# Routing matrix built between the expert-up tiles, and the up products parked in DRAM until the first down pass

## The reference, cut to what matters

```
qry = (hc @ w_query).reshape(-1, 8, 2, 128)
s = einsum('chpk,pnk->chpn', qry, sub_keys)
s1, i1 = top_k(s[:, :, 0], 16);  s2, i2 = top_k(s[:, :, 1], 16)
cand_s = s1[..., :, None] + s2[..., None, :]
top_s, pos = top_k(cand_s, 16)                 # 128 picks of a token
idx  = take_along_axis(i1 * 128 + i2, pos)
gate = softmax(top_s)
act  = gelu(einsum('cd,chkd->chk', hc, expert_u[idx]))
out  = einsum('chk,chkd->cd', gate * act, expert_v[idx])
```

## Time and profile before

| | us |
|---|---|
| median of 3 runs (2500.84 to 2504.45) | 2502.86 |
| the profiled execution, its own time | 2502.85 |
| its span in the profile | 2500.9 |
| PE busy, share of the span | 2391.2 (96%) |
| DVE, ACT, POOL busy | 1705.2, 1425.6, 193.2 |

### The profile page before, as it was taken

The page is one execution under the profiler, slowest core; times in us unless marked ns, Lnnn a source line. Parts: engine busy times, 40 slices in busy tenths (PEclk is TensorE's granted clock), DMA queues, the critical chain, the costliest instruction groups (busy, mean ns, idle before and its releaser), DMA issues. The chain is left out here.

```text
span 2500.9 us, 59673 instructions
## 1 busy us (share of the span) xinstructions
PE 2391.2 (96%) x19183; PEld 2338.6 (94%) x19183; DVE 1705.2 (68%) x3328; ACT 1425.6 (57%) x2560; POOL 193.2 (8%) x194
## 2 busy tenths in 40 slices
PE   8999999999999999999999999857999999999997
PEld 7999889989999999999999999756999999999997
DVE  7774688877776677777775444698666666666665
ACT  6444455556554566666666666765555555555553
POOL 0321000020110000000000000285000002000000
PEclk9999999999999999999999999899999999999999
DMA  6887444455664455555555555301666665566663
GB/s 215 288 300 240 154 150 136 135 173 173 184 209 158 153 172 179 171 177 175 175 170 182 179 183 183 111 0 58 214 181 179 182 178 169 181 179 182 179 182 119
DMA packets 121906, 431.95 MB, mean 173 GB/s; under 512 B 14568, under 2 KB 18920, under 8 KB 121584
## 3 DMA queue, kind: packets, MB, share of 16 engines
q1 hardware_dynamic: 116048, 410.08, 52.5%
q0 software_dynamic: 5792, 21.01, 2.3%
HBM read 423.28 MB, written 7.76 MB: 172 GB/s over the span
## 5 line engine op out<-in xcount | busy, mean ns | idle before, releaser
L262 DVE TENSOR_TENSOR lo<-raw,hi 128x512 fp32r<-128x512 f32 x1504 | 1034.3, 696 | 502.9 <-ACT hi L257 474.6
L257 ACT CAST hi<-raw 128x512 fp32r<-128x512 f32 x1504 | 908.9, 618 | 484.2 <-PE ps L277 359.2
L275 PE MATMUL ps<-h_hi,hi 128*128 128x264 f32 (+1 forms) x3200 | 920.4, 288 | 23.2 <-DVE lo L262 21.7
L277 PE MATMUL ps<-h_hi,lo 128*128 128x264 f32 (+1 forms) x3200 | 912.3, 285 | 0.0
L276 PE MATMUL ps<-h_lo,hi 128*128 128x264 f32 (+1 forms) x3200 | 912.1, 285 | 0.0
L275 PEld LDWEIGHTS ps<-h_hi,hi 128*128 128x128 f32 x3200 | 603.6, 189 | 38.7 <-DVE lo L262 24.1
L276 PEld LDWEIGHTS ps<-h_lo,hi 128*128 128x128 f32 x3200 | 604.0, 189 | 0.0
L277 PEld LDWEIGHTS ps<-h_hi,lo 128*128 128x128 f32 x3200 | 601.4, 188 | 0.0
L1730 PE MATMUL ps<-w_hi,hi 128*128 128x264 f32 x2048 | 584.3, 285 | 4.4 <-DVE x L1712 2.4
L1731 PE MATMUL ps<-w_lo,hi 128*128 128x264 f32 x2048 | 582.0, 284 | 0.0
L1732 PE MATMUL ps<-w_hi,lo 128*128 128x264 f32 x2048 | 581.7, 284 | 0.0
(11 more groups left out here) (264 smaller groups left out, 2317.3 us busy)
## 6 DMA issues: line engine op xcount, KB each, us to landing
raw<-u_tiles SPq DMA_DIRECT2D x256, 512.0 KB, 3.6
raw<-expert_v SPq DMA_DIRECT2D x256, 512.0 KB, 5.0
raw<-weights SPq DMA_DIRECT2D x240, 512.0 KB, 3.5
qb<-q_spill POOLq DMA_DIRECT2D x8, 512.0 KB, 7.7
x<-xT SPq DMA_DIRECT2D x4, 560.0 KB, 6.8
kvT<-qkv SPq DMA_DIRECT2D x1, 2240.0 KB, 12.6
x<-xT SPq DMA_DIRECT2D x1, 2240.0 KB, 8.7
x_spill<-x SPq DMA_DIRECT2D x1, 2112.0 KB, 8.7
```

The costliest lines, as they stand in the source:

```text
L257: nc.scalar.copy(hi[k % SPLIT][:], raw_quarter(k)).then_inc(hi_done, 1)
L262: nc.vector.tensor_tensor(lo[k % SPLIT][:], raw_quarter(k), hi[k % SPLIT][:].bitcast(F32), ALU.subtract).then_inc(lo_done, 1)
L275: pe.matmul(out, a, rh, start=start and j == 0, stop=False)
L277: m = pe.matmul(out, b, rh, start=False, stop=stop and j == QT - 1)
```

## The change: what it does

- The routing stage as a block disappears. Softmax (`soft_first`, `soft_second`), the exponential on ACT and the transposes go between the quarters of up pair `PAIR_R` (the 41st) and the one after it. The groups follow in the last 22 up pairs: 60 of them in 20 pairs, three to a pair (`G_AT`: behind quarters 0, 3 and 5), then four more in the last two pairs. Groups 64 and 65 are left for after the last tile.
- The product of a group is copied into `W` (`keep`) and not multiplied into it, since the up products are no longer there: gelu writes to one of two staging buffers `ust`, and POOL stores each tile to DRAM (`u_spill`) with a DMA of 128 x 264 numbers, 132 KB. POOL waits for each store to land before it issues the next one. The gelu of a pair waits for the store of the same buffer of the pair before (`u_free`).
- The one-hot matrices of the groups in the up pass live in the last 24 columns of `W` (`left_hot`, `right_hot`). One matrix is `W[:, :, c]`: its 128 numbers of a partition stand 264 numbers (1056 bytes) apart. Three sets of them, a ring, are in use. All right matrices are made by DVE; POOL makes none.
- In the first down pass SP loads each tile back into one of four buffers `urg`, and DVE multiplies it into `W[:, n, :]` (`times_u`) one chunk ahead of its use. In the second pass nothing is loaded.
- Some small constants change places in memory, so that the buffers fit.

```diff
-GS = 6
+GT, GR, GB = 4, 3, 6
+GP = 20
+MADE = GT * GR * GP
...
+    ust = [place(f"ust{b}", at["rows"] + 1056 * b, [P, LIVE]) for b in range(2)]
...
+    urg = place("urg", at["fin_r"], [P, 4, LIVE])
+    u_dram = nc.dram_tensor("u_spill", [NK, P, LIVE], F32, kind="Internal").ap()
...
+    PAIR_R = PAIR_QRY + PH * HEAD_PAIRS
+    PAIR_G = PAIR_R + 2
+    LEFT = (MADE + GT * 4) // GT
+    GROUPS = LIVE // GT
+    G_AT = (0, 3, 5)
+    MAKE_AT = (2, 5, 7)
...
+    def left_hot(b, t):
+        return W[:, :, MADE + 2 * GT * (GR - 1 - b) + t]
+    def right_hot(b, t):
+        return W[:, :, MADE + 2 * GT * (GR - 1 - b) + GT + t]
...
+            sp.wait_ge(mm_done, 8 * PAIR_U + SPLIT)
+            for b in range(2):
+                sp.wait_ge(u_free[b], NK // 2)
+            for s in range(4):
+                sp.dma_start(urg[:, s], u_dram[s]).then_inc(u_in[s], 16)
+        @block.gpsimd
+        def _(pool):
+            for b in range(2):
+                pool.sem_inc(u_free[b], 1)
+            with pool.Fori(0, NK // 2) as i:
+                for b in range(2):
+                    pool.wait_ge(tile_free[b], i + PAIR_QRY + 2)
+                    nc.gpsimd.dma_start(u_dram[2 * i + b], ust[b][:]).then_inc(u_out[b], 16)
+                    pool.wait_ge(u_out[b], 16 * i + 16)
+                    pool.sem_inc(u_free[b], 1)
...
+            def gelu(i, b):
+                act.wait_ge(u_free[b], i - PAIR_QRY + 1)
+                nc.scalar.activation(ust[b][:], ps[:, b, 0:LIVE], ACT.Gelu_apprx_tanh).then_inc(tile_free[b], 1)
+            def make(n, tok, out):
+                for t in range(2):
+                    nc.scalar.activation(out(t), iota[:], ACT.Square,
+                                         bias=chT[:, 3, bass.ds(tok + t, 1)]).then_inc(sq_done, 1)
+                for t in range(2):
+                    act.wait_ge(sq_done, 2 * n + t + 1)
+                    m = nc.scalar.activation(out(t), out(t), ACT.Relu, scale=-2.0,
+                                             bias=chT[:, 2, bass.ds(tok + t, 1)])
+                m.then_inc(l_act, 1)
...
+            with act.Fori(0, GP - 1) as p:
+                i = p + PAIR_G
+                for k in range(8):
+                    split_hi(act, 8 * i, AHEAD + k)
+                    if k in MAKE_AT:
+                        b = MAKE_AT.index(k)
+                        ring_make(GR * p + GR + b, b)
+                    if k % 4 == 3:
+                        tile_done(act, i, k // 4)
+                        gelu(i, k // 4)
...
+            def group(n, bank, lefts, rights):
+                pe.wait_ge(l_ready, n + 1)
+                pe.wait_ge(l_act, n + 1)
+                pe.wait_ge(g_used, n + 1)
+                for t in range(GT):
+                    m = pe.matmul(ps[:, bank, NK * t:NK * t + NK], lefts(t), rights(t), start=True, stop=True)
+                m.then_inc(g_ready, 1)
+            with pe.Fori(0, GP // 2) as p:
+                for u in range(2):
+                    i = 2 * p + u + PAIR_G
+                    for c in range(2):
+                        pe.wait_ge(tile_free[c], i + 1)
+                        for r in range(4):
+                            quarter_products(pe, 8 * i, 4 * c + r, ps[:, c, 0:LIVE], h2, QT * r, LIVE, r == 0, r == 3)
+                            if 4 * c + r in G_AT:
+                                b = G_AT.index(4 * c + r)
+                                group(2 * GR * p + GR * u + b, 2 + GR * u + b,
+                                      lambda t: left_hot(b, t), lambda t: right_hot(b, t))
...
+            def keep(n, bank):
+                dve.wait_ge(g_ready, n + GR + 1)
+                nc.vector.tensor_copy(W[:, :, bass.ds(GT * n, GT)], ps[:, bank, :].rearrange("p (t n) -> p n t", t=GT))\
+                    .then_inc(g_used, 1)
...
+                        split_lo(dve, 8 * i, AHEAD + k)
+                        if k in MAKE_AT:
...
+                            keep(n, 2 + GR * u + b)
+                            ring_make(n + GR, b)
...
                         load_half(sp, C0 + 4 * i + s, s, expert_v[0, 4 * i + s])
+                        sp.wait_ge(w_mul, 4 * i + s - 3)
+                        sp.dma_start(urg[:, s], u_dram[4 * i + s]).then_inc(u_in[s], 16)
...
+            def times_u(i, k):
+                n = 4 * i + k
+                dve.wait_ge(u_in[k % 4], 16 * (i + k // 4) + 16)
+                nc.vector.tensor_tensor(W[:, n, :], W[:, n, :], urg[:, k % 4], ALU.mult).then_inc(w_mul, 1)
```

More of the change, by code:

```diff
@@ new lines, in ring_make @@
+            def ring_make(n, b):
+                act.wait_ge(g_ready, n + 1 + late(n))
+                act.sem_inc(act_go, 1)
+                make(n, GT * n, lambda t: left_hot(b, t))
+            act_pairs(act, PAIR_QRY, PAIR_R, lambda i: gelu(i, 0), lambda i: gelu(i, 1))
+            for i in (PAIR_R, PAIR_R + 1):
+                for k in range(8):
+                    split_hi(act, 8 * i, AHEAD + k)
+                    if i == PAIR_R and k == 2:
+                        act.wait_ge(soft, 2)
+                        nc.scalar.activation(chosen[:, 2], chosen[:, 2], ACT.Exp).then_inc(soft_act, 1)
+                    if i == PAIR_R + 1 and k == 0:
+                        act.wait_ge(ch_done, 4)
+                    if i == PAIR_R + 1 and k in MAKE_AT:
+                        ring_make(MAKE_AT.index(k), MAKE_AT.index(k))
+                    if k % 4 == 3:
+                        tile_done(act, i, k // 4)
+                        gelu(i, k // 4)
@@ new lines, in _ @@
+            with act.Fori(0, GP - 1) as p:
+                i = p + PAIR_G
+                for k in range(8):
+                    split_hi(act, 8 * i, AHEAD + k)
+                    if k in MAKE_AT:
+                        b = MAKE_AT.index(k)
+                        ring_make(GR * p + GR + b, b)
+                    if k % 4 == 3:
+                        tile_done(act, i, k // 4)
+                        gelu(i, k // 4)
+            for i in range(PAIR_G + GP - 1, PAIR_U):
+                for k in range(8):
+                    split_hi(act, 8 * i, AHEAD + k)
+                    for n, b in LAST_MAKES.get((i - PAIR_G - GP, k), ()):
+                        ring_make(n, b)
+                    if k % 4 == 3:
+                        tile_done(act, i, k // 4)
+                        gelu(i, k // 4)
@@ L1417, in _ @@
+            act.wait_ge(mm_done, 8 * PAIR_U + SPLIT)
+            for n in range(LEFT, GROUPS):
+                make(n, GT * n, lambda t: lhot[:, n - LEFT, t])
         @block.tensor
         def _(pe):
-            pe_pairs(pe, PAIR_QRY, PAIR_U, h2, LIVE)
+            pe.sem_inc(g_ready, GR)
+            pe.sem_inc(g_used, GB)
+            pe_pairs(pe, PAIR_QRY, PAIR_R + 1, h2, LIVE)
+            pe.wait_ge(soft, 5)
+            for t in range(TT):
+                n = (P, P, DEC)[t]
+                for q in range(3):
+                    m = pe.transpose(ps[:, 2 + q, P * t:P * t + n],
+                                     chosen[0:n, q, t].rearrange("p h k -> p (h k)"), ident[0:n, 0:n])
@@ new lines, in _ @@
+            for i in range(PAIR_G + GP, PAIR_U):
+                for c in range(2):
+                    pe.wait_ge(tile_free[c], i + 1)
+                    for r in range(4):
+                        quarter_products(pe, 8 * i, 4 * c + r, ps[:, c, 0:LIVE], h2, QT * r, LIVE, r == 0, r == 3)
+                        for n, b in LAST_GROUPS.get((i - PAIR_G - GP, 4 * c + r), ()):
+                            group(n, 2 + n % GB, lambda t: left_hot(b, t), lambda t: right_hot(b, t))
+            for n in range(LEFT, GROUPS):
+                group(n, 2 + n % GB, lambda t: lhot[:, n - LEFT, t], lambda t: rhot[:, n - LEFT, t])
@@ L1507, in _ @@
                 assert split[0] == 8 * HEAD_PAIRS and count[0] == STEPS, (split[0], count[0], STEPS)
[L1508 to L1568, removed]
-                for q in range(3):
[L1570 to L1614, removed]
-                m.then_inc(l_ready, 1)
-            def weigh(i, b):
-                dve.wait_ge(g_ready, GS + GS * i + b + 1)
-                wv = W[:, :, bass.ds(4 * GS * i + 4 * b, 4)]
-                nc.vector.tensor_tensor(wv, wv, ps[:, 2 + b, :].rearrange("p (t n) -> p n t", t=4),
-                                        ALU.mult).then_inc(g_used, 1)
-            for b in range(GS):
-                hots(0, b)
-            with dve.Fori(0, GROUPS // GS - 1) as i:
-                for b in range(GS):
-                    weigh(i, b)
-                    hots(i + 1, b)
-            for b in range(GS):
-                weigh(GROUPS // GS - 1, b)
@@ new lines, in transposed, with make @@
+            def transposed():
+                dve.wait_ge(tr_ready, 1)
+                for q in range(3):
+                    nc.vector.tensor_copy(chT[:, q, :], ps[:, 2 + q, 0:LIVE]).then_inc(ch_done, 1)
+                dve.wait_ge(ch_done, 3)
```

(55 more changed lines are left out.)

100 lines of the change are left out of this document (70 added, 30 removed).

## The result

The changed kernel takes 2513.89 us (median of 7 runs, 2507.61 to 2515.99) against 2500.84 for the kernel before (7 runs, 2495.28 to 2504.45): a ratio of 1.0056, 95% interval 1.0045 to 1.0067. It is slower by about half a per cent, where 2462 us had been forecast.

What follows compares the result with a forecast made beforehand. PE's instructions were taken to bound both passes. From 2502.85 us, 119.6 for the gap came off; 75.5 for groups, 2.3 for transposes and 1 for joints were added: 2462.05, say 2462 us, range 2445 to 2516.

Steps and rivals of the forecast that it cites:

- part 2: 64 groups on PE's path in the up pass: 1.18 us each, 75.5 us in all (57 to 165).
- rival 1: PE pays for strided group operands, kernel slower: 2507 us at 0.087 a record, 2552 with both operands; chance 0.21.
- The DVE row: DVE reading 128 numbers: 279 ns side by side, 366 at 64 bytes' distance, 87 ns more; used for upper ends.
- The prediction's estimate from that page: If the 16-byte line rule doubled every PE group record: 512 x 0.111 = 57 us higher, 2519 us.
- the change of kind: PE going between up matmuls and float32 group matmuls: 0.29 us a group, taken from the query tiles' period.
- rival 4: Changing between matmul kinds costs nothing between long runs: 64 x 0.29 = 19 us less, 2443 us; chance 0.05.
- Part 1: Gap between up and first down pass: routing stage goes, 8.1 us of 127.7 stay, saving 119.6 us.
- the slow start: PE restarting after idling before the last two groups: 1.5 to 1.8 us a group and not 0.9.
- Part 3: DVE, ACT and POOL keep up in the up pass: DVE 10.7 us, ACT 9.0 of a 15.1 us pair; cost zero.
- rival 2: POOL's store chain sets the clock of the first 40 pairs, beyond 5.8 us a tile: 2511 us; chance 0.07.
- Part 4: Small things: nine transposes on PE's path 2.3 us, reloads in the first down pass zero, unseen joints 1 us.
- Rival 3: DVE or ACT delays splits in pairs with groups, or a late reload stalls the down pass: 2475 to 2494; chance 0.12.

Runs made afterwards that it cites:

- blocks: The changed kernel with W stored by groups of four tokens, so each one-hot matrix is 128 numbers side by side; 2443.73 us, ratio 0.9767 to the kernel before.
- both8: As blocks, but left and right matrices both interleaved, 8 bytes from number to number; 2451.37 us, a single run.
- one_product: The changed kernel with PE making only the first of a group's four products, spread over the four tokens; all matrices still made; 2419.12 us.
- blocks_x2: As blocks, but the 2.1 MB load of x2 in the first down pass cut into eight; 2440.29 us, ratio 0.9756 to the kernel before.

## Why the prediction was wrong

- **The step that failed** is the choice in part 2: "I take 75.5", a group at 1.18 us. It measured 1.99, 127.5 us in all, 52 us more. The other terms err by 1 us together (-0.3, -1.9 and +1.2), so this is nearly the whole distance between the forecast 2462.05 and the profiled execution's 2512.79. It turned a forecast gain of 41 us into a loss. The range (2445 to 2516) does hold the result, close to its upper end, since it took in the lower part of rival 1; the way the time would move was forecast wrong. The mechanism was named as rival 1, with a break-even of 0.080 us a record; the records are 0.238 apart, 0.127 above the 0.111 of the kernel before. Rival 1's own prices (2507 and 2552) hold the result between them, but it had a chance of 0.21.
- **Why the choice was wrong.** The ground for it was that a float32 record spends two cycles on a column and so leaves room for a slow read. The runs show that it leaves none: from 0.111 us side by side (blocks) the record goes to 0.227 to 0.238 with either operand at 16 bytes, or both at 16 or at 1056. The DVE row was the only strided row that the prediction had, it pointed the right way, and I set it aside because it was not PE's. It was too low as a price (0.087 a read of 128 numbers, from two lines that also write 8 sums and 16; PE's is 0.116 to 0.127), and the way it was added up was wrong too: moving and weights do not add, the slower counts.
- The Trainium skill, SBUF — State Buffer, in its note on SBUF cachelines, says that two hits to a 16-byte line give full bandwidth. By that rule both8 agrees, 0.118 us at 8 bytes against 0.236 at 16. The prediction's estimate from that page (each record doubled, 2519 us) was the nearest of all, in part by luck: it put the strides at 57 us where they cost 65 (512 x 0.127), and it kept 0.29 us a group for the change of kind, where 0.09 is left (1.99 - 8 x 0.238).
- **A second size in the same term** erred the other way. The 0.29 us for the change of kind, taken from the query tiles, is nothing between up matmuls (blocks: 0.898 us for eight records). That was rival 4, and without the strides the time would have been below the forecast: 2444. The trace of the kernel before says where the 0.29 stands. Behind the six records that start at 747.65 come

```profile
748.50 0.39 PE L275 MATMUL ps<-raw_hi,hi 128*128 128x264 f32 x1
748.72 0.29 PE L276 MATMUL ps<-raw_lo,hi 128*128 128x264 f32 x1
```

  so the six take 0.85 us to the next up matmul, and the eight of blocks 0.81. The four records of full width follow one another at 0.107 to 0.112 us, the first of them 0.120 behind the tile's matmul: going over to them costs nothing. The last two records have eight weight columns (the third matmul of L1270). 0.09 us stand ahead of them (0.205 from the fourth record to the fifth) and 0.19 behind (0.43 from the last record to the tile's second matmul, 0.24 in blocks). So the 0.29 belongs to the narrow matmul, which a group doesn't have; why a narrow one costs this was not tested.
- **Part 1 was right** in its sum: 7.78 us stay against 8.1. Inside it two errors offset each other. The two groups ran 2.74 us for 16 records, faster than the slow start I had put. That start was the clock: in the kernel before PE stood still for 4.7 us at a granted clock of 0.50 (the lower level, 1.2 GHz) and had 0.61 in the 6.1 us of the 32 records; here it stood for 1.8 us and had 0.81 in the 2.8 us of the two groups. The turn of the blocks, from the end of the last copy to the first down matmul, took 2.24 us against 1.68.
- **Part 3 was right.** In a pair with groups DVE waits 1.6 to 2.4 us for `hi` before three of its eight splits, PE waits for no `lo`, and one_product shows room down to 13.3 us. DVE is busy for 11.1 us of a pair (10.7 forecast) and ACT for 9.6 (9.0). POOL's chain is far from its bound: the stores land in 2.0 us at the median (4.3 at most) where 4.5 had been estimated from a 32 KB store's 4.1; rival 2 never came near.
- **Part 4**: transposes and joints took 1.4 us, not 3.3. The nine transposes take 1.0 us between two up matmuls (0.11 from start to start where they are of full width); their 1.96 in the earlier trace rows was at a granted clock of 0.50. The reload was put at zero and costs 1.2 us, by one stall behind the x2 load; blocks_x2 took it away. Rival 3 is right in kind there, and a tenth of its size. Of the signs, "pairs of 11.6 us up to the 41st" holds but for every fifth, which takes 13.5 in the kernel before too.

## What to carry to other kernels

When a stage moves onto the path of the engine that sets the pace, price its instructions as they will read there, not as they read before: a borrowed place in memory can double them. Look at the innermost distance of every PE operand, weights and moving alike, and mend both: one alone took 0.36 or 0.53 us off a pair of 17.58, both together 3.29. If the only strided row in a profile is another engine's, it is still evidence, and the range and the chances should lean on it. Here a layout by blocks, at no cost to its other readers, turned 0.6% slower into 2.3% faster.

## What the runs showed of the hardware

- A float32 matmul record of 128 columns takes 0.111 us with operands side by side, 0.118 with 8 bytes from number to number in both, 0.227 (moving) or 0.233 (weights) with 16 in one, 0.236 with 16 in both and 0.238 with 1056 in both, at a granted clock of 1.00 (2.4 GHz).
- DVE and ACT pay too, less. Mean durations in the pairs with groups, changed kernel first, blocks second:

```profile
L1677 DVE TENSOR_TENSOR W<-iota,chT 128x512 f32<-128x512 f32 x43 | 47.9, 1114 | 0.0
L1478 ACT ACTIVATE W<-W,chT 128x128 f32<-128x128 f32 x86 | 42.8, 549 | 0.0
```
```profile
L1699 DVE TENSOR_TENSOR W<-iota,chT 128x512 f32<-128x512 f32 x50 | 34.0, 680 | 0.0
L1491 ACT ACTIVATE W<-W,chT 128x128 f32<-128x128 f32 x100 | 34.0, 388 | 0.0
```

  For 512 numbers written 1056 bytes apart DVE takes 1114 ns and not 680, and ACT 549 and not 388 for 128 read and written so. Runs of four numbers (16 bytes) cost neither anything: 2048 bytes apart w_hi and w_lo read them at 413 and 433 ns (413 and 439 side by side), and 1056 bytes apart DVE's copy `keep` writes them in 684 ns (683 side by side).
- Going from the up pass's matmuls to the float32 ones of a group and back costs PE 0.01 us in all where the operands lie side by side (0.898 - 8 x 0.111), and 0.09 where they stand 1056 bytes apart (1.99 - 8 x 0.238).
